# Squares by column half at each norm, a token-ordered last product, outputs stored by quarter

## The reference

```python
def rms_norm(x, g):
    xf = xf * lax.rsqrt(jnp.mean(xf * xf, axis=-1, keepdims=True) + EPS)
    return (xf * g.astype(jnp.float32)).astype(x.dtype)
...
for layer in range(DEPTH):
    h = rms_norm(x, attn_norm_g[layer])
    z = h @ w_in[layer]
    ...
    x = x + jnp.concatenate([conv_out, attn_out], axis=-1) @ w_out[layer]
    h = rms_norm(x, ffn_norm_g[layer])
    if layer % 2 == 0:
        x = x + swiglu(h, dense_w1[i], dense_w3[i], dense_w2[i])
    else:
        x = x + moe_swiglu(h, router_w[i], moe_w1[i], moe_w3[i], moe_w2[i])
```

## Time and profile before

| | us |
|---|---|
| median of 3 runs | 1496.34 |
| lowest and highest run | 1492.58, 1497.39 |
| the profiled execution | 1495.59 |
| its span, first to last instruction | 1493.8 |
| PE busy in it | 1463.0 |

### The profile page before, as it was taken

One profiled execution on the slowest core, in us unless ns is written; L12 is line 12 of the kernel. 1 busy time (PEld: TensorE's weight loads), 2 busy tenths in 40 slices (PEclk: granted clock), 3 DMA queues, 4 the chain that ended last, 5 costly groups with the idle time before them and its releaser, 6 DMA issues.

```text
span 1493.8 us, 18648 instructions
## 1 busy us (share of the span) xinstructions
PE 1463.0 (98%) x7274; PEld 1177.1 (79%) x7274; DVE 1176.7 (79%) x1137; ACT 889.5 (60%) x804; POOL 32.2 (2%) x46
## 2 busy tenths in 40 slices
PE   7999999998999999999999999999999999999997
PEld 6654899997654888888888888888888888888886
DVE  3995544543995688898888898989889888889886
ACT  1144443331035577777777777776777777777774
POOL 1011000000010000000000000000000000000000
PEclk9999999999999899999999999999999999999999
DMA  7560755532350799999999999999999999999992
GB/s 241 166 229 0 246 194 185 193 113 88 124 186 1 280 376 368 371 362 353 368 335 368 376 353 374 357 342 362 368 370 363 354 375 332 365 375 363 368 369 110
DMA packets 203563, 426.59 MB, mean 286 GB/s; under 512 B 7378, under 2 KB 48594, under 8 KB 203476
## 3 DMA queue, kind: packets, MB, share of 16 engines
q1 hardware_dynamic: 202160, 424.90, 78.9%
q10 hardware_dynamic: 1316, 0.49, 0.1%
HBM read 424.31 MB, written 1.05 MB: 285 GB/s over the span
## 4 chain that ended last, share of the span: by engine, by line
PE 96%; DVE 1%; ACT 1%; issue 1%; POOL 1%; DMA 0%; POOLq 0%; SPq 0%; DVEq 0%; ACTq 0%
PE bank L1729 14%; PE bank L1731 14%; PE bank L1730 14%; PE bank L1295 8%; PE bank L1751 7%; PE bank L1753 7%; PE bank L1752 7%; PE bank L1470 3%; PE bank L1637 3%; PE bank L1638 3%; PE bank L1639 3%; PE bank L1739 2%; PE bank L1655 1%; PE bank L1654 1%; PE bank L1653 1%; PE bank L1681 1%
## 5 line engine op out<-in xcount | busy, mean ns | idle before, releaser
L832 DVE TENSOR_TENSOR w_split<-ring,w_split 128x2048 fp32r<-128x2048 f32 x369 | 843.9, 2291 | 188.7 <-ACT w_split L540 187.1
L540 ACT CAST w_split<-ring 128x2048 fp32r<-128x2048 f32 x369 | 706.5, 1915 | 294.4 <-PE bank L1731 161.5
L1729 PE MATMUL bank<-w_split,xe_hi 128*128 128x512 f32 x896 | 355.0, 396 | 0.0
L1731 PE MATMUL bank<-w_split,xe_lo 128*128 128x512 f32 x896 | 349.7, 390 | 0.0
L1730 PE MATMUL bank<-w_split,xe_hi 128*128 128x512 f32 x896 | 349.0, 389 | 0.0
L1731 PEld LDWEIGHTS bank<-w_split,xe_lo 128*128 128x128 f32 x896 | 168.1, 188 | 36.3
L1729 PEld LDWEIGHTS bank<-w_split,xe_hi 128*128 128x128 f32 x896 | 168.3, 188 | 35.1 <-DVE w_split L832 1.2
L1730 PEld LDWEIGHTS bank<-w_split,xe_hi 128*128 128x128 f32 x896 | 168.5, 188 | 33.2
L1751 PE MATMUL bank<-w_split,actT_hi 128*128 128x512 f32 x448 | 175.2, 391 | 0.0
L1753 PE MATMUL bank<-w_split,actT_lo 128*128 128x512 f32 x448 | 174.5, 389 | 0.0
L1752 PE MATMUL bank<-w_split,actT_hi 128*128 128x512 f32 x448 | 174.4, 389 | 0.0
(11 more groups left out here) (222 smaller groups left out, 1258.2 us busy)
## 6 DMA issues: line engine op xcount, KB each, us to landing
ring<-in_moe_w SPq DMA_DIRECT2D x336, 1024.0 KB, 5.7
ring<-in_dense_w SPq DMA_DIRECT2D x33, 1024.0 KB, 5.4
ring<-in_w_in SPq DMA_DIRECT2D x8, 1024.0 KB, 10.1
ring<-in_w_in SPq DMA_DIRECT2D x4, 2048.0 KB, 7.7
ring<-in_w_out SPq DMA_DIRECT2D x4, 2048.0 KB, 12.8
ring<-in_cmp_k_w SPq DMA_DIRECT2D x2, 2048.0 KB, 13.3
ring<-in_cmp_v_w SPq DMA_DIRECT2D x2, 2048.0 KB, 19.2
ring<-in_w_in SPq DMA_DIRECT2D x2, 1120.0 KB, 12.5
```

What stands on the lines that cost most here:

```text
L540: nc.scalar.copy(split_part(0, t), raw(t)).then_inc(w_hi_ready, 1)
L832: V.tensor_tensor(split_part(1, t), raw(t), split_part(0, t).bitcast(F32), ALU.subtract).then_inc(w_lo_ready, 1)
L1729: T.matmul(dst, xe_hi[:, kk, own], hi[:, k, :], start=(kk == 0), stop=False)
L1731: last = T.matmul(dst, xe_lo[:, kk, own], hi[:, k, :], start=False, stop=(kk == KD - 1))
```

## The change

- Each norm squares and sums by column half into a small table (`half_ms`), already divided by 1024; `mean_square` on DVE adds the two halves, and stands apart from `scaled_rows`.
- x is awaited by token half. For m = 0 the wait for the parameters (`par_loaded`) stands ahead of the second half's scaling, since the first half's gain now comes before it.
- The last `down` runs all of token half 0 first and signals `dense_done`; `normalise(2)` begins with that and waits for `w_used` only ahead of the second half's adds. `glu_product` and the dense `up` start with three of the four quarters and wait for the fourth halfway.
- For m = 1 the second half's mean moves ahead of both low splits, its scaling ahead of the second.
- Unread transposes: 12 new ones after the last `down`, 24 become 6 in the seam of m = 2, 12 and 12 become 5 and 3 at the router.
- The scatter goes by column half and waits for each half of the low part; the last `add_back` counts `token_added`, and SP stores each quarter of 256 KB after its add. The memset at the end goes; one of `slot_weight` in the router's tail, with its count, comes.

```diff
-            def square_sum(m, i):
+            def square_sum(m, i, n):
...
-                nc.scalar.activation(hn[:, i, :], x_sb[:, i, :], ACT.Square,
-                                     accum_out=ss[:, i:i + 1]).then_inc(ss_ready, 1)
+                if m == 0:
+                    sc.wait_ge(x_loaded[i], 16)
+                else:
+                    sc.wait_ge(x_ready, 4 * (m - 1) + NH * i + n + 1)
+                part = slice(n * BANK, (n + 1) * BANK)
+                nc.scalar.activation(hn[:, i, part], x_sb[:, i, part], ACT.Square, scale=D ** -0.5,
+                                     accum_out=half_ms[:, i, n:n + 1]).then_inc(ss_ready, 1)
...
-                square_sum(2 * l + 1, 0)
+                square_sum(2 * l + 1, 0, 0)
+                square_sum(2 * l + 1, 0, 1)
+                square_sum(2 * l + 1, 1, 0)
                 if l == 0:
                     split_tokens(0, 0)
-                square_sum(2 * l + 1, 1)
+                square_sum(2 * l + 1, 1, 1)
...
+            def mean_square(m, i):
+                dv.wait_ge(ss_ready, NH * (NT * m + i + 1))
+                V.tensor_scalar(ss[:, i:i + 1], half_ms[:, i, 0:1], half_ms[:, i, 1:2], EPS, ALU.add,
+                                ALU.add).then_inc(ms_ready, 1)
...
             def normalise(m):
-                for i in range(NT):
-                    for n in range(NH if m > 0 else 0):
-                        add_to_x(2 * n + i, i, n).then_inc(x_ready, 1)
-                    scaled_rows(m, i)
+                if m > 0:
+                    dv.wait_ge(dense_done, 1)
+                    for n in range(NH):
+                        add_to_x(2 * n, 0, n).then_inc(x_ready, 1)
+                mean_square(m, 0)
+                if m > 0:
+                    dv.wait_ge(w_used, BASE)
+                    for n in range(NH):
+                        add_to_x(2 * n + 1, 1, n).then_inc(x_ready, 1)
+                scaled_rows(m, 0)
+                mean_square(m, 1)
                 if m == 0:
                     dv.wait_ge(par_loaded, 48)
-                for i in range(NT):
-                    gained(m, i)
+                gained(m, 0, 0)
+                scaled_rows(m, 1)
+                gained(m, 0, 1)
+                gained(m, 1)
...
                 projected(0, 1)
+                mean_square(m, 0)
                 scaled_rows(m, 0)
                 projected(1, 0)
                 gained(m, 0, 0)
                 projected(1, 1)
                 gained(m, 0, 1)
+                mean_square(m, 1)
                 if l == 0:
                     split_low(0, 0)
+                scaled_rows(m, 1)
+                if l == 0:
                     split_low(0, 1)
-                scaled_rows(m, 1)
                 gained(m, 1)
...
             for l in range(L):
+                if l > 0:
+                    keep_busy(4, 12)
                 transpose_rows(2 * l, 0)
                 if l > 0:
                     pe.wait_ge(x_ready, 4 * (2 * l - 1) + 1)
-                    keep_busy(0, 24)
+                    keep_busy(0, 6)
                 transpose_rows(2 * l, 1)
-                pe.wait_ge(hT_ready, 4 * (2 * l + 1))
+                pe.wait_ge(hT_ready, 4 * (2 * l) + 3)
...
                     keep_busy(3, 20)
-                    pe.wait_ge(hTs_ready, 4)
+                    pe.wait_ge(hTs_ready, 3)
...
+                        order = [(f, n, i) for f in range(2) for n in range(NH) for i in range(NT)]
+                        if g == NDG - 1:
+                            order.sort(key=lambda o: o[2])
...
+                            if end and (n, i) == (NH - 1, 0):
+                                last.then_inc(dense_done, 1)
...
-            keep_busy(2, 12)
+            keep_busy(2, 5)
             pe.wait_ge(chosen_ready, 1)
...
-            keep_busy(2, 12)
+            keep_busy(2, 3)
             pe.wait_ge(sel_ready, NT * PAIR)
...
                 pe.wait_ge(selT_ready, nth(j, 2, 0))
-                pe.wait_ge(ye_lo_ready, nth(j, NH, 0))
                 for q, b in enumerate(BACK):
-                    i, n = divmod(q, 2)
+                    n, i = divmod(q, NT)
+                    if i == 0:
+                        pe.wait_ge(ye_lo_ready, nth(j, NH, n + 1))
...
-            sp.wait_ge(trips_done, 1)
-            for i in range(NT):
-                sp.dma_start(out[i * P:(i + 1) * P, :], x_sb[:, i, :]).then_inc(stored, 16)
+            for q in range(NT * NH):
+                n, i = divmod(q, NT)
+                sp.wait_ge(token_added, q + 1)
+                sp.dma_start(out[i * P:(i + 1) * P, n * BANK:(n + 1) * BANK],
+                             x_sb[:, i, n * BANK:(n + 1) * BANK]).then_inc(stored, 16)
```

More of the change, by code:

```diff
@@ L227, in hymba_trunk @@
         bank = [ctx.enter_context(nc.psum_tensor(f"bank{b}", [P, BANK], F32)) for b in range(8)]
-        x_loaded, par_loaded = sem("x_loaded"), sem("par_loaded")
+        x_loaded, par_loaded = [sem(f"x{i}_loaded") for i in range(NT)], sem("par_loaded")
         glu_arrived = [sem(f"glu{h}_arrived") for h in range(2)]
@@ L1193, in _ @@
             link(V.memset(pos_tab[:, :, PASSES * E:], -1.0))
+            V.memset(slot_weight[:], 0.0).then_inc(ye_lo_ready, NH)
             dv.wait_ge(count_psum, 1)
@@ L1267, in _ @@
             scaled_low((pairs, 0))
-            add_back((pairs, 0))
-            dv.wait_ge(added, pairs * (PAIR * 4))
-            V.memset(cmx[:], 0.0).then_inc(trips_done, 1)
+            add_back((pairs, 0), token_added)
         @block.tensor
@@ L1290, in transpose_rows, with product @@
                     last.then_inc(hT_psum, 1)
-            def product(dst, lhs, rhs, chunks):
+            def product(dst, lhs, rhs, chunks, upper=None):
                 for n, k in enumerate(chunks):
+                    if upper and n == KD // 2:
+                        pe.wait_ge(*upper)
                     last = T.matmul(dst, lhs(k), rhs(k), start=(n == 0), stop=(n == len(chunks) - 1))
@@ L1319, in glu_product @@
                         last = product(bank[GLU_BANK[c]][:, half * S:(half + 1) * S],
-                                       lambda k: w[:, k, c * P:(c + 1) * P], lambda k: hT[:, k, :], range(KD))
+                                       lambda k: w[:, k, c * P:(c + 1) * P], lambda k: hT[:, k, :], range(KD),
+                                       (hT_ready, 4 * (2 * l + 1)) if c == 0 and half == 0 else None)
                     last.then_inc(glu_psum, 1)
@@ L1636, in up @@
                             for k in range(KD):
+                                if k == KD // 2:
+                                    pe.wait_ge(hTs_ready, 4)
                                 T.matmul(dst, hi[:, k, c], hT_hi[:, k, :], start=(k == 0), stop=False)
@@ L1646, in down @@
                         hi, lo = split_views(t, 2)
-                        for f in range(2):
+                        order = [(f, n, i) for f in range(2) for n in range(NH) for i in range(NT)]
+                        if g == NDG - 1:
+                            order.sort(key=lambda o: o[2])
+                        for f, n, i in order:
                             first, end = g == 0 and f == 0, g == NDG - 1 and f == 1
-                            for n in range(NH):
-                                c = slice(n * BANK, (n + 1) * BANK)
-                                for i in range(NT):
-                                    dst, r = bank[2 * n + i][:], slice(i * P, (i + 1) * P)
-                                    T.matmul(dst, dact_hi[:, g % 2, f, r], hi[:, f, c], start=first, stop=False)
-                                    T.matmul(dst, dact_hi[:, g % 2, f, r], lo[:, f, c], start=False, stop=False)
-                                    last = T.matmul(dst, dact_lo[:, g % 2, f, r], hi[:, f, c], start=False, stop=end)
+                            c = slice(n * BANK, (n + 1) * BANK)
+                            dst, r = bank[2 * n + i][:], slice(i * P, (i + 1) * P)
+                            T.matmul(dst, dact_hi[:, g % 2, f, r], hi[:, f, c], start=first, stop=False)
+                            T.matmul(dst, dact_hi[:, g % 2, f, r], lo[:, f, c], start=False, stop=False)
+                            last = T.matmul(dst, dact_lo[:, g % 2, f, r], hi[:, f, c], start=False, stop=end)
+                            if end and (n, i) == (NH - 1, 0):
+                                last.then_inc(dense_done, 1)
                         last.then_inc(w_used, 1)
```

23 lines of the change are left out of this document (9 added, 14 removed).

## The result

The changed kernel takes 1481.08 us at the median of six executions (1480.86 to 1487.75), the kernel before beside it 1495.5: the ratio is 0.9909, with a 95% interval of 0.9899 to 0.992. It is 0.9% faster, and the time lies inside the range given (1481 to 1490.5), though at its very edge: the gain is 14.4 and not 9.8. The profiled execution took 1480.86 (span 1479.1). A second set of six executions, taken later beside the kernel before (1495.86), had its median at 1485.84 (1483.26 to 1491.24), ratio 0.9939 (0.9922 to 0.9956). The two intervals don't meet: executions of one and the same kernel differ by several us, and most of that is where the clock falls, as the table shows.

A forecast was written before the change was run, and what follows sets the result against it. PE makes up 96% of the chain, so only its idle, unread or low-clock work and the end count. Gains of 6.2 + 1.1 + 0.3 + 2.4 - 0.2 = 9.8 us from 1495.59 give 1485.8, range 1481 to 1490.5.

The forecast's parts named there:

- Norm after the dense mixer: Wait between last dense product and layer 2's first product: 6.2 us less, bounds 7 and 3.
- Rival 1: Clock falls at the norm after the dense mixer anyway; gain there 3, whole about 1489.0; chance 0.13.
- Norm before it: Norm before the dense mixer: product starts 1.1 us earlier, or 1.7 if POOL is not held up.
- the 0.69 that I added: Norm before the dense mixer: POOL's power assumed to wait out the split beside it, 0.69 us.
- over 1 us: Expected sign at the norm before the dense mixer: POOL's power beside a split lasts over 1 us.
- End: Scatter by halves 0.8 earlier plus quarter stores saving 1.6: 2.4 us gained, between 0.8 and 4.1.
- I take 0.2 lost: Start: earlier transposes against parameter wait and PE gaps; 0.2 us lost, bounds 0.8 gained, 1.7 lost.
- when it is met: Start: DVE's parameter wait, now ahead of the second scaling; nothing in the trace showed its time.
- the positions, the selection and the split of the rows ... come 1.5 us earlier: Router: five unread transposes instead of 12 bring this work 1.5 us earlier; 0.3 us gained in all.
- Rival 2: Router's clock rises where it did, shorter fillers gain 1.8, start neutral; whole about 1484.1; chance 0.22.
- keeps its instructions, and I leave it at its time: Convolution, attention, mixer and expert products, outside the five changed places: assumed unchanged in time.
- Rivals 3 and 4: Low clock into first expert, near 1501, chance 0.02; dense seam bound by something thought hidden, about 1492.0, chance 0.03.

The follow-up runs named there:

- the kernel before with the end alone: Kernel before with only the change's scatter by halves and quarter stores at the end: 1493.69 us, ratio 0.9986.
- the filled one: Changed kernel plus unread transposes at the start (11) and POOL's power of layer 0 (16), router rows back to 12 and 12: 1480.51 us, ratio 0.9896.
- router rows back: Changed kernel with the router's two rows of unread transposes set back from 5 and 3 to 12 each: 1488.53 us, ratio 0.9931.
- the norm's order: Changed kernel, norm before the dense mixer: second half scaled ahead of both splits, 12 unread transposes instead of 20: 1487.84 us, ratio 0.9936.
- last product unsorted: Changed kernel with the last dense product in its old order, column half before token half: 1489.85 us, ratio 0.9952.

## Why the prediction held, point by point

**Norm after the dense mixer: right** (6.2 forecast, 6.61 measured, bounds 3 to 7). The first product came 5.6 us after the last dense matmul's end, as forecast, at the full clock. Of the 6.6, the sort of the last product gives 1.5, as its own run shows, and up to 2.1 is the row of 24, much of it at the half clock, that held up the second half's transposes (350.87 to 352.99), as the trace before shows. The rest, about 3, no run takes apart: squares by half, the full clock in the real transposes, the wait for three quarters. The unread rows that stay add little to the stretch itself (0.08 and 0.16) but keep 1.1 that would be lost behind it. Rival 1 did not come: in ten profiles with these rows the clock never fell at this place, in both without them it did, at 344 and 349. The rule of the Trainium skill that spoke for that rival ("TensorE: Matmul & The Clock Gate", Part 4: PE-mode transpose, that transposes do not count as PE being busy) does not agree with these traces: rows that consist only of transposes kept the full clock here and at POOL's power, and brought the full pace sooner at the start. These are float32 transposes, which the profile lists as MATMUL with the identity; whether another form would behave otherwise no run here shows.

**Norm before it: right in kind, 1.49 for 1.1.** The power is held up by the split (0.94 beside it, 0.56 without), but by 0.38 and not the 0.69 that I added: the split had begun 0.16 before the power, so at most the rest of it, 0.52, could count. The forecast sign "over 1 us" was wrong. Most of the other difference is the row: I let the product wait for its whole listed time, but it began at 159.03 and the row is listed until 159.28. What ends this stretch, the unread row, was right.

**End: right** (2.4 forecast; 2.55, and 2.54 by itself). The tail saves 1.8 where I took 1.6. That this came out is partly luck: I halved between fixed delay and transfer, while 0.6 of it is the earlier issue of the last store, which the sum did not hold.

**Start: mis-sized.** The step "I take 0.2 lost" failed. The mechanism named there, idle gaps of PE and a late full pace, is what happens, and the wait for the parameters was "when it is met" at 10.76, behind the router's small load. It costs 0.5 to 2.2 by the start's end (35.18 before; 35.64 to 37.35 in the seven profiles), 1.3 on their mean, nearer the bound of 1.7 than the value taken; one profile passes that bound.

**Router: the size was wrong, and the reason too.** The step "the positions, the selection and the split of the rows ... come 1.5 us earlier" rested on 12 transposes at the half clock. At the full clock the 12 end before the choice is known, so cutting them brings nothing, while the gaps left by the cut let the clock fall in the gather: 0.9 lost. That second half the prediction had. The stretch still got 2.9 shorter in the first profile (1.4 in the second), because the clock was low for less of it: 3.4 us in the first, all of it in the gather, and 6.8 in the second, 10.2 before. Why it stayed up among the first profile's routing products isn't shown. Rival 2, the cut paying in full, is refuted, although the first median lies closer to its 1484.1 than to the forecast. The squares by half brought 0.37, near the 0.25 taken: the kernel before with the end alone and the filled one, with the same rows and 3.4 us low among the routing products, differ by just that (20.89 and 20.52).

**Not in the sum: the clock in code that isn't touched.** The step "keeps its instructions, and I leave it at its time" failed at POOL's power of layer 0: -1.65 in the first profile, +1.43 in the second. That and the router are why the first median fell 4.7 below the forecast, where it stayed in the range by luck, 0.08 from its end, and the second met it (1485.84 for 1485.8); the second match is partly luck as well, since a start that lost more and a power that lost more stand against a router that gained more than forecast. Rivals 3 and 4 did not come: the low clock ended ahead of the experts in every profile, and the dense seam paid.

## What to carry to other kernels

Where a change is worth a few us and PE's clock falls in several places, compare stretches over several profiles before believing a median: here the same kernel gave 1481.1 and 1485.8. Fill the idle times of PE behind which the clock falls (here of 1.6 to 2.2 us) with work that fits into them, also in code that the change doesn't touch; size the row at the full clock, since a row that looks too long at the half clock may fit at the full one. A wait that is moved ahead of other work on an engine takes the latest of all loads that share its semaphore.

## What the chip showed that was not expected

**A slower pace at the full clock.** Two profiles (router rows back, and the norm's order) ran the whole dense mixer 4.6 us slower, 185.3 for 180.65, with the granted clock at 1.00. The windows of 165 to 330 us, of the router variant and then of the changed kernel, count the matmuls:

```profile
165.00:330.00 165.00, 165.00 (x1198) 155.95 (x1197) 80.93 (x50) 67.06 (x50) 0.00 (x0) 1.00 0.53 172
```

```profile
165.00:330.00 165.00, 165.00 (x1229) 155.90 (x1229) 82.15 (x51) 68.10 (x52) 0.00 (x0) 1.00 0.53 175
```

2.5% fewer in the same time, with PE busy throughout and nearly the same DMA traffic. Records can be missing from a trace, but the length of the stretch says the same. A third profile (last product unsorted) was slower only from 159 to 185. It came with kernels that differ only elsewhere, and its cause is open; executions of 1488 and more are likely of this kind, which isn't shown, since only profiles tell.

**The granted clock at the start reads 1.00** while the first transposes take 0.24 each and the first products 0.42, about twice what they take later: for the first microseconds the pace of the matmuls is the thing to read.

**A 32 KB load that lands last.** The router's weights, which ACT issues and not SP, went out at 2.48 behind 444 KB of other parameters, took 8.27 us to land and held up DVE's first gain until 10.76.
